# Eight gate tile loads of a Strassen-blocked projection: another place in GpSimd's order, and one of them into another buffer

## The reference, cut to what matters

```python
def merge_ffn(x, o_a, o_b, g_a, g_b, w_proj_gmlp, w_proj_nsa, w_out, g_mlp_norm, w_up, w_down):
    mix = jax.nn.sigmoid(g_a) * (o_a @ w_proj_gmlp) + jax.nn.sigmoid(g_b) * (o_b @ w_proj_nsa)
    x = x + mix @ w_out
    hm = rmsnorm(x, g_mlp_norm)
    return x + jnp.square(jax.nn.relu(hm @ w_up)) @ w_down
```

## Time and profile before

| | |
|---|---|
| median of 3 runs | 2592.0 us (2591.44 to 2592.83) |
| the profiled execution | 2593.7 us, its span in the profile 2592.2 us |
| PE busy in the span | 2567.7 us (99%) |
| DVE, ACT, POOL busy | 2019.8, 1449.5, 474.0 us |
| the projection's stretch | about 928 to 1104 us |

### The profile page before, as it was taken

One profiled execution on the slowest core, in us unless ns is written; L12 is line 12 of the kernel. 1 busy time (PEld: TensorE's weight loads), 2 busy tenths in 40 slices (PEclk: granted clock), 3 DMA queues, 4 the chain that ended last, 5 costly groups with the idle time before them and its releaser, 6 DMA issues. The chain is left out here.

```text
span 2592.2 us, 56699 instructions
## 1 busy us (share of the span) xinstructions
PE 2567.7 (99%) x21295; PEld 2537.9 (98%) x21295; DVE 2019.8 (78%) x2903; ACT 1449.5 (56%) x2441; POOL 474.0 (18%) x641
## 2 busy tenths in 40 slices
PE   9999999999999999899999999999999999999998
PEld 9999999999999999899999999999999999999998
DVE  6456646668777788865688888888898888898888
ACT  6445436556444455532366656666566665666656
POOL 2001350001122221023202122121121211212113
PEclk9999999999999999999999999999999999999999
DMA  6633552214344467644336575665766756657568
GB/s 212 203 115 115 163 176 74 67 50 132 119 141 138 147 196 214 172 138 137 122 119 158 149 176 149 168 165 144 171 152 165 173 141 166 157 160 177 140 170 180
DMA packets 128089, 389.45 MB, mean 150 GB/s; under 512 B 14450, under 2 KB 16114, under 8 KB 127696
## 3 DMA queue, kind: packets, MB, share of 16 engines
q1 hardware_dynamic: 69328, 245.36, 28.1%
q0 software_dynamic: 55456, 136.73, 25.0%
q10 hardware_dynamic: 3168, 5.45, 0.6%
HBM read 302.77 MB, written 91.00 MB: 152 GB/s over the span
## 5 line engine op out<-in xcount | busy, mean ns | idle before, releaser
L3011 DVE TENSOR_TENSOR w_lo<-w_raw,w_hi 128x1024 fp32r<-128x1024 f32 x351 | 428.1, 1222 | 105.1 <-ACT w_hi L2027 104.2
L2027 ACT ACTIVATE w_hi<-w_raw 128x1024 fp32r<-128x1024 f32 x352 | 370.9, 1062 | 200.9 <-PE aux L1450 69.2
L1450 PE MATMUL aux<-at_t,w_hi 128*128 128x260 f32 x2016 | 368.4, 282 | 0.6 <-DVE w_lo L3011 0.5
L2204 DVE TENSOR_TENSOR w_lo<-w_raw,w_hi 128x512 fp32r<-128x512 f32 x216 | 158.9, 738 | 256.7 <-ACT w_hi L1595 255.9
L1514 PE MATMUL aux<-fb_mid,w_hi 128*128 128x260 f32 x1920 | 352.5, 284 | 1.4 <-DVE w_lo L3011 1.0
L1595 ACT ACTIVATE w_hi<-w_raw 128x512 fp32r<-128x512 f32 x216 | 135.3, 628 | 315.9 <-PE mm L1006 294.4
L1450 PEld LDWEIGHTS aux<-at_t,w_hi 128*128 128x128 f32 x2016 | 310.3, 188 | 1.3 <-DVE w_lo L3011 1.2
L1514 PEld LDWEIGHTS aux<-fb_mid,w_hi 128*128 128x128 f32 x1920 | 294.9, 188 | 2.7 <-DVE w_lo L3011 1.2
L1450 PE MATMUL aux<-at_t,w_lo 128*128 128x260 f32 x1008 | 284.2, 282 | 0.0
L1514 PE MATMUL aux<-fb_mid,w_lo 128*128 128x260 f32 x960 | 270.5, 282 | 0.0
L1514 PE MATMUL mm<-fb_mid,w_hi 128*128 128x260 f32 x1440 | 264.0, 282 | 0.0
(11 more groups left out here) (598 smaller groups left out, 6834.2 us busy)
## 6 DMA issues: line engine op xcount, KB each, us to landing
w_raw<-in_w_ff SPq DMA_DIRECT2D x256, 512.0 KB, 3.6
out_y_t<-y_mid POOLq DMA_DIRECT2D x120, 520.0 KB, 8.0
w_raw<-in_w SPq DMA_DIRECT2D x110, 512.0 KB, 3.6
w_raw<-in_w_st SPq DMA_DIRECT2D x88, 512.0 KB, 5.0
g_in<-merge_d POOLq DMA_DIRECT2D x8, 1040.0 KB, 9.4
w_raw<-in_w_st POOLq DMA_DIRECT2D x10, 512.0 KB, 5.3
st_sum<-in_w_st POOLq DMA_DIRECT2D x10, 512.0 KB, 5.4
merge_d<-z POOLq DMA_DIRECT2D x18, 260.0 KB, 3.7
```

The lines of the kernel that those rows point to most:

```text
L1450: last = pe.matmul(dst, w, at_of(j)[:, e:e + HT], start=FRESH[b] and j == 0 and part == 0, stop=j == KP - 1 and part == 2, skip_group_chec ...
L2027: run(hi_of(p, k), source(p, k), ACT.Copy).then_inc(ff_hi, 1)
L2204: dve.tensor_tensor(w_lo[:, c, :], raw(u, c), w_hi[:, c, :].bitcast(F32), ALU.subtract).then_inc(lo_split, 1)
L3011: dve.tensor_tensor(lo_of(p, k), source(p, k), hi_of(p, k).bitcast(F32), ALU.subtract).then_inc(ff_lo, 1)
```

## The change

All gate loads stand in another place of GpSimd's order. In a part, the order is now: `wide_sum(p)`; in part 0 the first half of the last gate tile; `low_sum(to)`; then the gates. Part 0 makes the second half of the last tile and loads the gates of part 0. Part 1 loads those of part 1, part 2 of part 2. Part 3 loads those of part 3 and, behind a wait for PE's last product of part 3, those of part 4, into a new buffer `g_late`, which lies in the second quarter of `a_hi` (an operand of parts 0 to 3). Parts 4, 5 and 6 load the gates of the following part. The waits (`gated`, `mix_lo`, `ff_used`) are set to fit. In the gate pairs (`part < 0`) the order is as before.

```diff
@@ -476,6 +476,7 @@
         mix_a = [at(f"mix_a{q}", [P, 4, TOK], mix_home[q]) for q in range(4)]
         g_in = [at("g_in0", [P, 4, TOK], i1), at("g_in1", [P, 4, TOK], r1)]
+        g_late = at("g_late", [P, 4, TOK], o1 + q_size)
@@ -757,7 +758,10 @@
         def gate_part(p, t_):
-            return g_in[p.part % 2][:, t_:4:2, :]
+            return gates_home(p)[:, t_:4:2, :]
+
+        def gates_home(p):
+            return g_late if p.part == N_PROJ // 2 else g_in[p.part % 2]
@@ -3493,7 +3497,7 @@
             def load_gates(p):
                 for t_ in range(2):
                     pool.wait_ge(g_stored[t_], 64 * (p.q + 1))
-                pool.dma_start(g_in[p.part % 2][:, :, :], merge_d.rearrange("(q k t) p n -> t q p k n", k=4, t=2)[
+                pool.dma_start(gates_home(p)[:, :, :], merge_d.rearrange("(q k t) p n -> t q p k n", k=4, t=2)[
                     p.phase][p.q]).then_inc(g_loaded[p.part % 2], 16)
@@ -3504,33 +3508,28 @@
                 p, old, to = Pair(n), Pair(n - 1), Pair(n + 1)
                 if p.loaded_sums:
                     wide_sum(p)
+                if p.part <= 0:
+                    gate_half(M_ST + n - 1, 0, st_out(old, 0))
                 if p.part < 0:
-                    gate_half(M_ST + n - 1, 0, st_out(old, 0))
+                    gate_half(M_ST + n - 1, 1, st_out(old, 1))
+                if p.part < N_PROJ - 1:
+                    low_sum(to)
                 if p.part == 0:
+                    gate_half(M_ST + n - 1, 1, st_out(old, 1))
                     pool.wait_ge(ff_used, old.used + NP)
                     load_gates(p)
-                if p.part == 4:
-                    pool.wait_ge(gated, KP + 6)
+                if p.part == 1:
+                    pool.wait_ge(mix_lo, GM_DONE)
                     load_gates(p)
-                if p.part > 4 and p.part < N_PROJ - 1:
-                    pool.wait_ge(gated, KP + 2 * p.part)
-                    load_gates(to)
-                if p.part < 0:
-                    gate_half(M_ST + n - 1, 1, st_out(old, 1))
-                if p.part == 0:
-                    pool.wait_ge(mix_lo, GM_DONE)
-                    load_gates(to)
-                    gate_half(MB - 1, 0, st_out(old, 0))
                 if p.part in (2, 3):
                     pool.wait_ge(gated, KP + 2 * p.part - 2)
                     load_gates(p)
-                if p.part == 4:
-                    pool.wait_ge(gated, KP + 8)
+                if p.part == 3:
+                    pool.wait_ge(ff_used, p.used + NP)
                     load_gates(to)
-                if p.part < N_PROJ - 1:
-                    low_sum(to)
-                if p.part == 0:
-                    gate_half(MB - 1, 1, st_out(old, 1))
+                if p.part in (4, 5, 6):
+                    pool.wait_ge(gated, KP + (8, 6, 12)[p.part - 4])
+                    load_gates(to)
```

## The result

The changed kernel takes 2600.1 us, median of 7 runs (2597.48 to 2603.39), beside 2592.16 (2591.40 to 2593.72, 7 runs) for the kernel before: ratio 1.0032, 95% interval [1.0021, 1.0043]. That is 8 us slower, where 1.8 us faster was forecast; it lies above the range too. The profiled execution took 2600.56 us, its span 2599.1.

The account below looks back on a forecast made before the run. PE, busy 99% of the span, was taken to bound the kernel. The terms -2.7 + 0.5 + 3.8 - 3.4 = -1.8 us gave 2590.2 us against 2592.0; own range 2587 to 2593.5, full range 2584.2 to 2596.5.

Parts of the forecast that it names:

- the two terms: Slot 0's weight load lands sooner: -2.7 us at part 1's b = 2, -3.4 us for parts 6 and 7.
- The mechanism of the loss: GpSimd's queue, parts 2 to 4: wide_sum waits behind gate loads; part 4's lands near 1030, holding PE up 4.1 us.
- rival (a): Summing transfers are not held up, as engines overlap them with the gates ahead: -7.6 us, 2584.4; chance 0.27.
- Rival (c): Slot 0 stays late because of wide_sum beside it, not the gates: +1.6 us, 2593.6; chance 0.08.
- the term for parts 2 and 3: One gate load ahead of each wide_sum: part 2 loses 0.5 us, part 3 comes out at its deadline, 0.
- the clock: A fall after part 1's new pause costs up to 1.7 us; left out of the sum, kept in the range.
- parts 4 and 5: Two gate loads delay part 4's wide_sum, so part 5's b = 2 starts later: +3.8 us, part 5's gain swallowed.
- Rival (b): A gate load holds its queue as long as seen, 4.4 us or more: +3.0 to +8.6, 2595.0 to 2600.6; chance 0.15.
- The prediction's own sign for (b): PE pauses over 1 us in part 2 or 3 would show the forecast wrong.
- the gate load between the sums: Parts 5 to 7: wide_sum is over 7 us behind low_sum, so one gate load fits between: 0.

Follow-up runs that it names:

- both_ends: Against the kernel before: gate loads of parts 0, 1, 5, 6 and 7 moved, parts 2 to 4 not, no g_late; 2588.29 us, ratio 0.9986.
- two loads put back: Against both_ends: gate loads of parts 3 and 4 behind low_sum of part 4, the latter into g_late; 2593.25 us, ratio 1.0004.
- experiments 7: Against the changed kernel: gate loads 1 to 4 bring two of their four tiles, used twice; 2591.09 us, ratio 0.9994.
- 8: Against the changed kernel: weight loads of slots 2 and 0 in parts 2 to 4 bring a quarter of their columns; 2596.78 us, ratio 1.0020.
- 9: Against the changed kernel: part 2's gate load, ahead of part 3's wide_sum, brings one tile instead of four; 2598.5 us, ratio 1.0024.
- split_four: Against both_ends: part 4's gate load cut into two of 520 KB, the second behind the gating of part 3; 2586.74 us, ratio 0.9980.
- late_three: Against the kernel before: only the gate loads of parts 5, 6 and 7 moved behind low_sum; 2589.29 us, ratio 0.9988.
- one_gate: Against both_ends: one load put back, part 2's gate load behind low_sum of part 3, ahead of its wide_sum; 2592.12 us, ratio 0.9999.
- split_four_b: Against split_four: gate load 0 behind wide_sum of part 1, ahead of load 1, instead of behind low_sum; 2587.24 us, ratio 0.9981.

## Why the prediction was wrong, point by point

**Gains.** In PE's timeline they came as worked out. Part 1's b = 2 gained 2.9 us (forecast 2.7), and parts 6 and 7 together 3.6 (3.4). In time, `both_ends` has 3.9 us (1.3 to 6.0) for the 6.1 of the two terms, so less may have reached the end than the sum took for granted. The pause of 1.5 us before part 1's b = 2 was foreseen at 1.7, and it lowered no clock here.

**The mechanism of the loss** was right as well, and rival (a) is out: a `wide_sum` behind gate loads waits, and part 4's pause was 3.90 us where 4.1 was forecast. Rival (c) is out by the gains.

**The step that failed** is the term for parts 2 and 3, "+0.5 us" and "Part 3 comes out at its deadline, 0". It lets `wide_sum` land 3.9 us after the gates ahead of it, with the engines otherwise worked out by bytes. The measure to compare is from `low_sum`'s issue to `wide_sum`'s landing (us). `low_sum` was issued at 973.01, 992.54 and 1012.73 before, so the forecast's landings (986.0; part 3's deadline 1013.80 - 2 x 2.89 - 2.35 = 1005.7; 1030) make 13.0, 13.1 and 17.3:

| kernel | part 2 | part 3 | part 4 |
|---|---|---|---|
| before | 11.0 | 10.5 | 11.7 |
| forecast | 13.0 | 13.1 | 17.3 |
| changed | 14.0 | 16.2 | 18.0 |
| loads on ACT's queue | 12.7 | 12.9 | 13.2 |
| one load put back | | 14.8 | |
| two loads put back | | | 17.5 |
| gate loads halved | 14.2 | 10.4 | 14.4 |
| weight loads light | 14.9 | 13.6 | 15.9 |

In part 3 the sum took 3.1 us more than forecast. Both the gate bytes ahead and the weight loads beside are in it (experiments 7, 8 and 9).

The forecast treated the 16 engines as one pool that works off its bytes, and most of the sum did move that way. What came late was its end: of the 128 packets of part 3's sum the 122nd began at 1008.07 and the last only at 1010.16, and in part 4 at 1035.20 and 1037.39. In the kernel before the last began 0.1 and 0.2 us behind the 122nd in the same parts. A sum has landed when its last packet has, so about 2 of the 3.1 us are these last six packets. SP's two weight loads were under way beside them and landed at 1011.2 and 1012.7. With those loads light the last packet of part 3 was only 0.6 us behind the 122nd. The trace doesn't say on which engines the late packets were, nor why on those.

**The margin moved too.** My deadlines for parts 2 and 3 were those of before. The gain in part 1 moves the due start of part 2's b = 5 ahead by 1.85 us (from 987.91 to 988.91 - 1.91 - 0.94), but `low_sum` of part 2 by 1.45 only (973.01 before, 972.50 less 0.94 after), and in part 3 `low_sum` comes 14.5 us ahead of b = 5's due start instead of 15.5. A slack is the difference of two moving times. So in part 2 the forecast 0.5 us, 1.0 more to the landing and 0.4 less slack make the pause of 1.9, and in part 3 3.1 more and 1.0 less slack make 4.1 of the 4.3. One load put back alone gave a pause of 1.93.

**What was left out of the sum:** the clock. I had priced its fall for the one new pause in front of part 1's b = 2, where it did not come, and not behind the two long ones, where it took 2.9 and 1.4 us. (The 1.4 took the place of a pause: the forecast left PE some 1.8 us of waiting before part 5's b = 2, from 1028.25 + 4.1 + 4 x 2.89 = 1043.9 to 1045.7, and none was left.) For part 4 it was open to me: a pause forecast at 4.1 us is longer than the 1.75 us one behind which the earlier trace rows show 0.72.

With these put right the sum reads -2.9 + 3.0 + 4.5 + 6.7 - 0.6 - 3.6 = +7.1 at part 7's b = 3. Held against the terms of the forecast, parts 2 and 3 gave +7.5 where +0.5 stood, the low clock behind part 3's pause +2.9 where nothing stood, parts 4 and 5 +3.3 (3.90 + 1.4 - 2.04) where +3.8 stood, and the gains -6.5 where -6.1 stood.

Rival (b), a gate load that holds its queue longer than its bytes, gave up to 2600.6, and that is where the time came out. The prediction's own sign for (b), pauses over 1 us in parts 2 and 3, was seen as well. In part 3 its direction is right. But the number is luck: at 2600.6 it has 9.0 us for part 4 alone, where 3.3 came, and no low clock; and light weight loads would not help if it were all.

**Still open.** How far landings scatter is to be seen in parts 6 and 7, where the order of the transfers is one and the same in the changed kernel and ten of the others. From `low_sum`'s issue the sum took 13.2 to 15.2 us in part 6 and 13.2 to 14.9 in part 7. So differences of under 2 us in the table are not told apart, and those of part 2 (13.0 forecast, 12.7 to 14.9 measured) are all of that size. Why light weight loads gave 14.9 there, and why in experiment 9 part 4's sum took 19.4 with nothing changed in its own loads, stays open. In parts 5 to 7, where the prediction put the gate load between the sums at 0, the sum landed in 6.7, 7.3 and 5.6 us, and no pause before b = 5 came of it.

## What to carry to other kernels

A bulk load that nothing waits for goes behind the urgent transfer of its queue, not directly ahead of the next one: a transfer of 5.3 us with one or two loads of 1 MB directly in front took 8 to 13. Where such a load fits no gap, it can be cut: in `split_four` an urgent load of the other queue then landed in 6.1 us instead of 7.6. A transfer has landed with its last packet: where two queues shared the engines, engine time added up by bytes came out about 2 us early. A forecast landing within 1 us of its deadline is worth an expected pause, not zero, and the deadline itself has to be moved by the gains forecast further ahead. Pauses like those of 3.2 us and more here are charged with the low clock behind them as well (1.4 to 3.0 us each).

## What the runs showed that I had not expected

The granted clock behind pauses: the pauses of 3.9 us and more (4.29, 3.90, 4.51, and 6.67 in experiment 9) were all followed by 0.50 for 2 to 6 us, which is 1.2 GHz, and cost 1.4 us or more, mostly 3. The 3.19 us of experiment 8 was followed by 0.50 over 3 us as well, while 2.79 us in part 2 of the same run left the clock at 1.00. Shorter ones went either way: 1.75 us in the kernel before was followed by 0.72, and 2.19 us in `late_three`, 1.79 and 2.11 in `one_gate` by 0.50 over 2 to 3 us, while pauses of 1.0 to 2.2 us elsewhere left it at full level. The seven runs of the changed kernel follow their mean clock too: 2597.48 us at 0.999, 2601.78 and 2603.39 at 0.997.

In the projection a summing transfer of 512 KB with no gate load ahead of it takes 5.0 to 5.7 us from issue to landing (twice more, 6.0 and 6.5, in `split_four_b`), with or without a gate load issued behind it in its own queue. With gate loads on another queue it took 6.8 to 8.3.
